# Latent attention on one core: rotated queries first, the query norm's root later, two value blocks to a PSUM bank

## The chip, the core and the metric

The kernel runs on one core of a Trainium2 chip. The metric is the device time of one execution in microseconds. Before the change the median of three runs is 2636.99 us (2633.98 to 2645.04).

## The reference

The program computes two blocks of layers on 512 tokens of width 1024, all in float32. The first is attention beside a state-space layer between two feed-forward layers; the second starts with latent attention (MLA), then layer norms, a convolutional feed-forward layer, a gated linear attention and again the same tail. The change touches the latent attention alone:

```python
def mla_mixer(x, positions, cos, sin, w_in, q_norm, kv_norm, w_uq, w_uk, w_uv, w_o):
    h = x @ w_in
    c_q, c_kv, k_r = jnp.split(h, [MLA_Q_LORA, MLA_Q_LORA + MLA_KV_LORA], axis=-1)
    c_q = rms_norm(c_q, q_norm)
    c_kv = rms_norm(c_kv, kv_norm)
    q = (c_q @ w_uq).reshape(B, S, MLA_HEADS, MLA_NOPE + MLA_ROPE)
    q_nope = q[..., :MLA_NOPE]
    q_rope = apply_rope(q[..., MLA_NOPE:], cos[:, :, None], sin[:, :, None])
    k_rope = apply_rope(k_r, cos, sin)
    k_nope = (c_kv @ w_uk).reshape(B, S, MLA_HEADS, MLA_NOPE)
    v = (c_kv @ w_uv).reshape(B, S, MLA_HEADS, MLA_V)
    scale = (MLA_NOPE + MLA_ROPE) ** -0.5
    ...
    s = (q_nope . k_nope + q_rope . k_rope) * scale, masked, softmax, times v
    ...
    return (o @ w_o).astype(x.dtype)
```

There are 16 heads, with 128 plain and 64 rotated columns in a query and 128 in a value; the query's latent width is 512, that of keys and values 256.

## The kernel before

Every product of float32 matrices is made of three: each operand is split into a high half (a cast by ScalarE to the matmul's format) and a low half (what is left, a subtraction by VectorE), and TensorE adds high x high, high x low and low x high into one PSUM bank (`mm3`, L581 to L583). So a result that is used as an operand again costs a cast on ScalarE and a subtraction on VectorE that both read its bank. Weights come by DMA from SP's queue into `raw`, and are split the same way into `uh` (L554, ScalarE) and `ul` (L569, VectorE), called in the code by `feed_hi` and `feed_lo`, some units ahead of their use.

The code is written out per engine: `latent_pe`, `latent_act` and `latent_dve` each loop over a step i and issue that engine's instructions in the order of the code, with semaphore waits between the engines. An engine never passes an instruction that waits. The steps are a pipeline over the 16 heads: step i has the scores of head i, the transposes of the probabilities of head i-2 and the output of head i-3. Each even step i below 16 starts with the queries and keys of pair p = i/2 of heads.

What TensorE does in an even step from 4 on (one pair, i even):

- `queries_pe`: the plain queries of both heads (`qn` 0 and 1, 12 products each), the rotated queries of both heads in one product (`qr`, 12), the keys of both heads (`kn` 0 and 1, 6 each);
- `latent_output_pe`: the output of head i-3 (`mo`, L2587, 4 products with the weight loads of float32 shown as 8);
- values of pair i/2 - 1, in four blocks of 128 tokens (`lin_tok`, 8 x 3 products of 256 columns), each block in a bank of its own;
- `latent_turn_pe`: ten transposes into three banks (L2559: four, four, two);
- `latent_scores_pe`: the scores of head i, five products for each of four token blocks, in banks 4 to 7.

Everything but the scores rotates through banks 0 to 3 (`bk.limit(4)`, `bk.take`): a group takes the next bank in turn, so it waits until the group four takes before it has been read by the engine that frees it. The readers and what frees a bank: `qn`: cast to `QNH` on ScalarE (L2450), then `QNL` on VectorE (L2474), which frees it. `qr`: four copies of 32 rows on ScalarE (`rope_act`, L2329) which swap the halves, then on VectorE the multiply by the cosine (L2336), which frees it, the multiply by the sine (L2338) and the sum (L2340); the result is cast to `QA` on ScalarE (L2462) and its low half made on VectorE (L2486), and the scores wait for that. `kn`: `KNH` (L2454), then `KNL` (L2479), which frees it. `mo`: `OH` (L2597), then `OL` (L2601), which frees it. Values: the copy to `VT` on ScalarE (L2498). Transposes: copies to `PTm` on VectorE (L2579) and ScalarE (L2577).

ScalarE and VectorE begin the step with the softmax of an earlier head (`latent_softmax_act` L2537; `latent_normalise_dve` L2543 and L2547, `latent_softmax_dve` L2527 and L2530), then the casts of `queries_act`, `OH`, then `queries_turned_act` (`QA`), the weights, `VT`, and `PTm`. In pair 0 the norm of the queries' latent is computed beside the queries: TensorE adds squares between the products (L2361), ScalarE takes the root (`query_norm_act`, L2392) and VectorE the inverse (L2423, L2425), which the softmax multiplies with. After step 10's values half of the output projection is done (`latent_project_pe`), and the other half behind the loop.

Of the kernel before, what the change touches and what calls it, by code (L numbers as in the profile page):

```python
# [22 lines left out]
H2 = [(0, 512)]  # L23
# [245 lines left out]
def program(nc, A, out):  # L269
    with ExitStack() as ctx:  # L270
# [10 lines left out]
        s_mm = tally("s_mm")  # L281

        s_whi, s_hi, s_fn, s_cp = (tally(n) for n in ("s_whi", "s_hi", "s_fn", "s_cp"))

        s_wlo, s_lo, s_par, s_dv = (tally(n) for n in ("s_wlo", "s_lo", "s_par", "s_dv"))
# [33 lines left out]
        bk = Banks(8)  # L319
# [219 lines left out]
        def feed_hi(e, name, ahead=1):  # L539

            u = done["act use"]
            assert units[u].name == name, (units[u].name, name)
            done["act use"] += 1
            ahead_hi(e, ahead)
# [12 lines left out]
        def feed_lo(e, name, ahead=1):  # L557

            u = done["dve use"]
            assert units[u].name == name, (units[u].name, name)  # L560
            done["dve use"] += 1
            ahead_lo(e, ahead)
# [10 lines left out]
        def next_unit(e, name):  # L573
            u = done["pe"]
            assert units[u].name == name, (units[u].name, name)
            done["pe"] += 1
            s_wlo.wait_ge(e, ("unit", u))
            return u

        def mm3(e, o, wh, wl, xh, xl, first, last):  # L580
            e.matmul(o, wh, xh, start=first, stop=False)  # L581
            e.matmul(o, wh, xl, start=False, stop=False)  # L582
            return e.matmul(o, wl, xh, start=False, stop=last)  # L583

        def lin(e, name, X, halves, key, xs=None, cols=None, u=None, frees=True, along=None):

            if u is None:
                u = next_unit(e, name)
            hi, lo, _ = halves_of(u)
            kc = units[u].kc  # L590
            w0, w1 = cols or (0, hi.shape[2])
            xh, xl, tag = X
            for hf, (t0, n) in enumerate(halves):
                b = bk.take(e, key + (hf,))
                for k in range(kc):
                    x = k if xs is None else xs[k]
                    s_lo.wait_ge(e, (tag, x))
                    if along:
                        along()
                    i = mm3(e, psum[0:w1 - w0, b, 0:n], hi[:, k, w0:w1], lo[:, k, w0:w1], xh[:, x, t0:t0 + n],  # L600
                            xl[:, x, t0:t0 + n], k == 0, k == kc - 1)
                ends = [("unit", u)] if frees and hf == len(halves) - 1 else []
                i.then_inc(*s_mm.up(key + (hf,), *ends))
            return u
# [168 lines left out]
        def P(key, n=512, parts=slice(0, 128)):  # L773
            return psum[parts, bk.of[key], 0:n]
# [1539 lines left out]
        def cq_over(e):  # L2314

            s_mm.wait_ge(e, ("cq", 3, 0))
            s_lo.wait_ge(e, ("xq", 3))
            s_fn.wait_ge(e, ("xq", "sq", 3))
# [4 lines left out]
        def rope_act(e, key):  # L2323

            s_mm.wait_ge(e, key)
            if key[0] == "qr" and key[1] > 2:
                s_dv.wait_ge(e, ("rope", "qr", key[1] - 3, 0))
            for k in range(4):
                e.copy(rope_tile(key)[32 * k:32 * k + 32, :], P(key, 512, slice(32 * (k ^ 1), 32 * (k ^ 1) + 32))).then_inc(  # L2329
                    *s_cp.up(("rope",) + key))  # L2330

        def rope_dve(e, key, dst):
            s = rope_tile(key)
            s_cp.wait_ge(e, ("rope",) + key)
            s_par.wait_ge(e, "trig")
            e.tensor_tensor(dst, P(key), COS[:, :], MUL).then_inc(*bk.free(s_dv, key))  # L2336
            s_dv.wait_ge(e, NOW)
            e.tensor_tensor(s, s, SIN[:, :], MUL).then_inc(*s_dv.up())  # L2338
            s_dv.wait_ge(e, NOW)
            e.tensor_tensor(dst, dst, s, ADD).then_inc(*s_dv.up(("rope",) + key))  # L2340
# [49 lines left out]
        def query_norm_act(e):  # L2390
            s_mm.wait_ge(e, "qss")
            e.activation(rq, P("qss", 4), ACT.Sqrt, bias=EPS5, scale=1.0 / 512).then_inc(*bk.free(s_fn, "qss", "qrt"))  # L2392
# [39 lines left out]
                e.tensor_tensor(HV[:, k, :], HV[:, k, :], R0, MUL).then_inc(*s_pool.up(("x0", k)))  # L2432

        def queries_pe(e, p, along=None):
            u = lin(e, "uq", XQ, H2, ("qn", p, 0), cols=(0, 128), frees=False)
            lin(e, "uq", XQ, H2, ("qn", p, 1), cols=(128, 256), u=u, frees=False)
            lin(e, "uq", XQ, H2, ("qr", p), cols=(256, 384), u=u)
            u = lin(e, "uk", XK, H2, ("kn", p, 0), cols=(0, 128), frees=False, along=along)
            lin(e, "uk", XK, H2, ("kn", p, 1), cols=(128, 256), u=u, along=along)

        def queries_act(e, p):
            feed_hi(e, "uq", 2)
            if p:
                s_mm.wait_ge(e, ("ms", 2 * p - 1))
            else:
                cq_over(e)
                s_pool.wait_ge(e, ("x0", 7))
            for hh in range(2):
                s_mm.wait_ge(e, ("qn", p, hh, 0))
                e.copy(QNH[:, hh, :], P(("qn", p, hh, 0))).then_inc(*s_hi.up(("qn", p, hh)))  # L2450
            rope_act(e, ("qr", p, 0))
            for hh in range(2):
                s_mm.wait_ge(e, ("kn", p, hh, 0))
                e.copy(KNH[:, hh, :], P(("kn", p, hh, 0))).then_inc(*s_hi.up(("kn", p, hh)))  # L2454
            if p == 0:
                query_norm_act(e)

        def queries_turned_act(e, p):
            s_dv.wait_ge(e, ("rope", "qr", p, 0))
            for hh in range(2):  # L2460
                rows = slice(64 * hh, 64 * hh + 64)
                e.copy(QA[rows, hh, :], QR[rows, :]).then_inc(*s_hi.up(("qr", p, hh)))  # L2462
            feed_hi(e, "uk", 1 if p == 1 else 2)

        def queries_dve(e, p):
            feed_lo(e, "uq", 2)
            if p:
                s_mm.wait_ge(e, ("ms", 2 * p - 1))
            else:
                cq_over(e)  # L2470
                s_lo.wait_ge(e, "KR")
            for hh in range(2):
                s_hi.wait_ge(e, ("qn", p, hh))
                e.tensor_tensor(QNL[hh][:, :], P(("qn", p, hh, 0)), QNH[:, hh, :].bitcast(F32), SUB).then_inc(  # L2474
                    *bk.free(s_lo, ("qn", p, hh, 0), ("qn", p, hh)))
            rope_dve(e, ("qr", p, 0), QR)
            for hh in range(2):
                s_hi.wait_ge(e, ("kn", p, hh))
                e.tensor_tensor(KNL[:, hh, :], P(("kn", p, hh, 0)), KNH[:, hh, :].bitcast(F32), SUB).then_inc(  # L2479
                    *bk.free(s_lo, ("kn", p, hh, 0), ("kn", p, hh)))  # L2480

        def queries_turned_dve(e, p):
# [4 lines left out]
                    *s_lo.up(("qr", p)))  # L2487
            feed_lo(e, "uk", 1 if p == 1 else 2)

        def latent_values_act(e, p):  # L2490
            feed_hi(e, "uv")
            if p:
                s_mm.wait_ge(e, ("mo", 2 * p - 1))
            else:
                cq_over(e)
            for i in range(4):
                s_mm.wait_ge(e, ("uv", p, i))
                e.copy(VT[:, i, :], P(("uv", p, i), 256)).then_inc(*bk.free(s_cp, ("uv", p, i), ("uv", p)))  # L2498

        def latent_scores_pe(e, h):  # L2500
            p, hh = h // 2, h % 2
# [148 lines left out]
        def latent_pe(e):  # L2650
            latent_first_pe(e)
            bk.limit(4)
            norm = query_norm_pe(e)

            def sums(n):
                for _ in range(n):
                    next(norm, None)

            for i in range(18):
                if i % 2 == 0 and i < 16:  # L2660
                    queries_pe(e, i // 2, None if i else lambda: sums(2))
                if i >= 3:
                    latent_output_pe(e, i - 3)
                if i == 0:
                    lin_tok(e, ("uv",), XK, [0, 128, 256, 384], 256, ("uv", 0), lambda: sums(1))
                if i % 2 == 0 and 4 <= i <= 16:
                    lin_tok(e, ("uv",), XK, [0, 128, 256, 384], 256, ("uv", i // 2 - 1))
                if i == 10:
                    latent_project_pe(e, 0)
                if 2 <= i <= 17:  # L2670
                    latent_turn_pe(e, i - 2)
                if i < 16:
                    latent_scores_pe(e, i)
            bk.limit(8, 4)
            latent_project_pe(e, 1)
            first_layer_pe(e, "h1", "x10", "mo", (OH, OL, "o1"), [("mproj", 1, k) for k in LAST], 0)
# [1051 lines left out]
```

## Time and profile before

| what | value |
|---|---|
| median of three runs | 2636.99 us |
| profiled execution | 2637.52 us |
| its span, first to last instruction | 2635.7 us |
| TensorE (PE) busy | 2573.6 us, 98% |
| its weight loads (PEld) busy | 2214.4 us, 84% |
| VectorE (DVE) busy | 1675.4 us, 64% |
| ScalarE (ACT) busy | 1051.2 us, 40% |
| GpSimd (POOL) busy | 352.6 us, 13% |
| mean DMA rate | 96 GB/s |
| granted TensorE clock, mean | 0.998 of full speed |

The span lies 1.8 us under the profiled execution's own time, and that 0.5 us over the median. The shares are means over stages of very different kinds: the heads' loop of the latent attention takes from about 1226 to 1503 us, with its output projection's first half in it. Within it a busy time of 98% says little: one must look for the idle time just ahead of an instruction, which stands in brackets behind its row together with the work that ended it.

### The profile page before, as it was taken

How to read it: one execution, taken by the hardware profiler on the slowest of the kernel's cores; microseconds unless marked ns; L12 is line 12 of the kernel's file. 1: busy time of each engine (PE TensorE's matmuls, PEld its weight loads, DVE VectorE, ACT ScalarE, POOL GpSimd, SP SyncE). 2: the span in 40 equal slices, each digit the busy share in tenths (PEclk: the TensorE clock that was granted, in tenths of full speed). 3: DMA queues.
4: the chain of work that ended last, by engine and by line, in shares of the span. 5: the costliest groups of instructions: out<-in, count | busy, mean ns of one | idle time of the engine just before them, and what ended most of it. 6: DMA issues, size and time to landing. Idle time of an engine off the chain costs nothing.

```text
span 2635.7 us, 35250 instructions
## 1 busy us (share of the span) xinstructions
PE 2573.6 (98%) x14532; PEld 2214.4 (84%) x14532; DVE 1675.4 (64%) x2597; ACT 1051.2 (40%) x1689; POOL 352.6 (13%) x385
## 2 busy tenths in 40 slices
PE   7999999999999999999999999999999999999999
PEld 7999999976688888887788798888898879888887
DVE  6865864468656534536775777747765477764765
ACT  4222333134434222235562545424454355433435
POOL 1143531220001000011000050000222014000031
PEclk9999999999999999999999999999999999999999
DMA  5243444631133233322121222332332222242322
GB/s 150 89 134 118 135 148 148 218 97 37 48 112 100 80 115 101 92 80 69 44 69 56 69 89 88 96 102 83 109 103 86 75 80 75 78 120 96 92 92 65
DMA packets 297687, 252.91 MB, mean 96 GB/s; under 512 B 20653, under 2 KB 286391, under 8 KB 297527
## 3 DMA queue, kind: packets, MB, share of 16 engines
q1 hardware_dynamic: 286055, 230.76, 27.9%
q0 software_dynamic: 7024, 17.74, 2.3%
q8 instruction: 115, 1.88, 0.3%
q10 hardware_dynamic: 4448, 2.16, 0.3%
q14 instruction: 45, 0.37, 0.0%
HBM read 235.06 MB, written 17.66 MB: 96 GB/s over the span
## 4 chain that ended last, share of the span: by engine, by line
PE 83%; DVE 10%; ACT 4%; issue 2%; POOL 1%; DMA 1%; SPq 0%; ACTq 0%; POOLq 0%; DVEq 0%
PE ps L581 25%; PE ps L582 25%; PE ps L583 25%; DVE ul L569 2%; ACT uh L554 1%; PE ps L2587 1%; PE ps L787 1%; PE ps L2559 1%; PE ps L1660 1%; PE ps L1902 0%; PE ps L2000 0%; DVE rbuf L802 0%; DVE HL L1153 0%; DVE tmp L1142 0%; DVE tmp L2978 0%
## 5 line engine op out<-in xcount | busy, mean ns | idle before, releaser
L569 DVE TENSOR_TENSOR ul<-raw,uh 128x1024 fp32r<-128x1024 f32 (+3 forms) x416 | 513.8, 1258 | 316.2 <-ACT uh L554 315.5
L581 PE MATMUL ps<-OH,uh 128*128 128x512 f32 (+1 forms) x1736 | 645.5, 372 | 4.5 <-DVE ul L569 3.8
L583 PE MATMUL ps<-OH,ul 128*128 128x512 f32 (+1 forms) x1736 | 638.5, 368 | 0.0
L582 PE MATMUL ps<-OL,uh 128*128 128x512 f32 (+1 forms) x1736 | 638.4, 368 | 0.0
L554 ACT CAST uh<-raw 128x1024 fp32r<-128x1024 f32 (+3 forms) x416 | 412.5, 1025 | 157.3 <-PE ps L583 116.9
L581 PEld LDWEIGHTS ps<-OH,uh 128*128 128x128 f32 x1736 | 327.3, 189 | 65.4 <-DVE ul L569 5.6
L582 PEld LDWEIGHTS ps<-OL,uh 128*128 128x128 f32 x1736 | 327.5, 189 | 54.8 <-issue 1.9
L583 PEld LDWEIGHTS ps<-OH,ul 128*128 128x128 f32 x1736 | 327.3, 189 | 54.6
L581 PE MATMUL ps<-HH,uh 128*128 128x512 f32 (+2 forms) x946 | 320.2, 338 | 4.0 <-DVE ul L569 2.9
L582 PE MATMUL ps<-HL,uh 128*128 128x512 f32 (+2 forms) x946 | 318.1, 336 | 0.0
L583 PE MATMUL ps<-HH,ul 128*128 128x512 f32 (+2 forms) x946 | 318.0, 336 | 0.0
L581 PE MATMUL ps<-XH,uh 128*128 128x264 f32 (+1 forms) x992 | 309.5, 312 | 6.2 <-DVE tmp L1146 2.5
L582 PE MATMUL ps<-XL,uh 128*128 128x264 f32 (+1 forms) x992 | 303.5, 306 | 0.0
L583 PE MATMUL ps<-XH,ul 128*128 128x264 f32 (+1 forms) x992 | 303.3, 306 | 0.0
L581 PEld LDWEIGHTS ps<-XH,uh 128*128 128x128 f32 x992 | 186.8, 188 | 25.9 <-issue 14.0
L581 PEld LDWEIGHTS ps<-HH,uh 128*128 128x128 f32 x946 | 178.9, 189 | 24.9 <-DVE ul L569 3.1
L582 PEld LDWEIGHTS ps<-HL,uh 128*128 128x128 f32 x946 | 179.0, 189 | 18.3 <-issue 0.5
L583 PEld LDWEIGHTS ps<-HH,ul 128*128 128x128 f32 x946 | 179.0, 189 | 18.2
L583 PEld LDWEIGHTS ps<-XH,ul 128*128 128x128 f32 x992 | 187.0, 189 | 8.4
L582 PEld LDWEIGHTS ps<-XL,uh 128*128 128x128 f32 x992 | 187.0, 189 | 7.1
L818 POOL TENSOR_TENSOR acc<-acc,tmp 128x512 f32<-128x512 f32 (+2 forms) x56 | 69.4, 1239 | 668.3 <-ACT tmp L808 664.0
L2752 POOL TENSOR_TENSOR acc<-H 128x512 f32<-128x512 f32 x4 | 8.6, 2147 | 939.3 <-DVE H L2991 621.2
(471 smaller groups left out, 3725.7 us busy)
## 6 DMA issues: line engine op xcount, KB each, us to landing
raw<-in_ffn_w SPq DMA_DIRECT2D x40, 1024.0 KB, 5.1
raw<-in_ffn_w_up SPq DMA_DIRECT2D x40, 1024.0 KB, 5.0
raw<-in_ffn_w SPq DMA_DIRECT2D x32, 704.0 KB, 4.3
raw<-in_ffn_w_down SPq DMA_DIRECT2D x32, 704.0 KB, 4.4
raw<-in_w_in SPq DMA_DIRECT2D x16, 1024.0 KB, 5.6
raw<-in_gla_w_in SPq DMA_DIRECT2D x12, 1024.0 KB, 5.0
raw<-in_mla_w_o SPq DMA_DIRECT2D x8, 1024.0 KB, 4.7
raw<-in_ple_w_gate SPq DMA_DIRECT2D x8, 1024.0 KB, 4.8
```

What stands on the lines that cost most here:

```text
L554: e.copy(h, src).then_inc(*s_whi.up((u, j)))
L569: e.tensor_tensor(l, src, h.bitcast(F32), SUB).then_inc(*s_wlo.up(("unit", u)))
L581: e.matmul(o, wh, xh, start=first, stop=False)
L582: e.matmul(o, wh, xl, start=False, stop=False)
L583: return e.matmul(o, wl, xh, start=False, stop=last)
L787: i = e.matmul(psum[:, b, 0:n], ones[:, :], tile[:, t0:t0 + n], start=j == 0, stop=j == len(parts) - 1)
L818: e.tensor_tensor(a, a, tmps[k - 1][:, t0:t0 + n], ADD).then_inc(*s_pool.up(*((tag, "acc", k, hf) for hf in hfs)))
L1660: t = e.matmul(psum[:, b, 66 * g:66 * g + 66], w[:, 128 * g:128 * g + 128], UB[q][:, e0 + g, :], start=True, stop=True)
L2559: t = e.transpose(psum[:, b, o:o + 128], SS[h % 2][:, SO[n] + 128 * k:SO[n] + 128 * k + 128], ident[:, :])
L2587: t = e.matmul(psum[:, b, 128 * k:512], VT[:, k, 128 * (h % 2):128 * (h % 2) + 128], PTm[:, PO[k]:PO[k] + 512 - 128 * k], start=k == 0, st ...
L2752: e.tensor_tensor(a, HV[:, 0, :], HV[:, 1, :], ADD).then_inc(*s_pool.up((xt, "two")))
```

## The change

Three edits, all in the loop over pairs of heads. First, `qr` is made ahead of `qn` 0 and 1 on TensorE, and read ahead of them on ScalarE and VectorE (`rope_act` and `rope_dve` stand first). Second, the root of the query norm moves on ScalarE from behind pair 0's key casts to behind its `QA` casts. Third, two blocks of values share a bank (`latent_values_pe`): the unit, the products and their sizes stay, but only two banks are taken and `VT` is filled by two copies of 512 columns in place of four of 256.

```diff
         def queries_pe(e, p, along=None):
-            u = lin(e, "uq", XQ, H2, ("qn", p, 0), cols=(0, 128), frees=False)
-            lin(e, "uq", XQ, H2, ("qn", p, 1), cols=(128, 256), u=u, frees=False)
-            lin(e, "uq", XQ, H2, ("qr", p), cols=(256, 384), u=u)
+            u = lin(e, "uq", XQ, H2, ("qr", p), cols=(256, 384), frees=False)
+            lin(e, "uq", XQ, H2, ("qn", p, 0), cols=(0, 128), u=u, frees=False)
+            lin(e, "uq", XQ, H2, ("qn", p, 1), cols=(128, 256), u=u)
...
         def queries_act(e, p):
             feed_hi(e, "uq", 2)
+            if p == 0:
+                cq_over(e)
+                s_pool.wait_ge(e, ("x0", 7))
+            rope_act(e, ("qr", p, 0))
             if p:
                 s_mm.wait_ge(e, ("ms", 2 * p - 1))
-            else:
-                cq_over(e)
-                s_pool.wait_ge(e, ("x0", 7))
             for hh in range(2):
                 s_mm.wait_ge(e, ("qn", p, hh, 0))
                 e.copy(QNH[:, hh, :], P(("qn", p, hh, 0))).then_inc(*s_hi.up(("qn", p, hh)))
-            rope_act(e, ("qr", p, 0))
...
-            if p == 0:
-                query_norm_act(e)

         def queries_turned_act(e, p):
...
+            if p == 0:
+                query_norm_act(e)
             feed_hi(e, "uk", 1 if p == 1 else 2)

         def queries_dve(e, p):
             feed_lo(e, "uq", 2)
+            if p == 0:
+                cq_over(e)
+                s_lo.wait_ge(e, "KR")
+            rope_dve(e, ("qr", p, 0), QR)
             if p:
                 s_mm.wait_ge(e, ("ms", 2 * p - 1))
-            else:
-                cq_over(e)
-                s_lo.wait_ge(e, "KR")
             for hh in range(2):
                 s_hi.wait_ge(e, ("qn", p, hh))
...
-            rope_dve(e, ("qr", p, 0), QR)
...
+        def latent_values_pe(e, p, along=None):
+            u = next_unit(e, "uv")
+            hi, lo, _ = halves_of(u)
+            xh, xl, tag = XK
+            for j in range(2):
+                b = bk.take(e, ("uv", p, j))
+                for a in range(2):
+                    t0 = 256 * j + 128 * a
+                    for k in range(2):
+                        s_lo.wait_ge(e, (tag, k))
+                        if along:
+                            along()
+                        t = mm3(e, psum[:, b, 256 * a:256 * a + 256], xh[:, k, t0:t0 + 128], xl[:, k, t0:t0 + 128],
+                                hi[:, k, 0:256], lo[:, k, 0:256], k == 0, k == 1)
+                t.then_inc(*s_mm.up(("uv", p, j), *([("unit", u)] if j else [])))
...
-            for i in range(4):
-                s_mm.wait_ge(e, ("uv", p, i))
-                e.copy(VT[:, i, :], P(("uv", p, i), 256)).then_inc(*bk.free(s_cp, ("uv", p, i), ("uv", p)))
+            for j in range(2):
+                s_mm.wait_ge(e, ("uv", p, j))
+                e.copy(VT[:, 2 * j:2 * j + 2, :].rearrange("p a n -> p (a n)"), P(("uv", p, j))).then_inc(
+                    *bk.free(s_cp, ("uv", p, j), ("uv", p)))
```

How the order of instructions changes, at three places. Line numbers behind the new function are 17 higher in the changed kernel.

ScalarE, pair 0, from the weight casts to the copies of the values (`misc` is the norm's column, `tmp` the rotation's tile):

```order
 L554 CAST uh<-raw_53 128x512
-L2450 CAST QNH<-ps 128x512 x2
 L2329 COPY tmp_65<-ps 32x512 x4
+L2451 CAST QNH<-ps 128x512 x2
 L2454 CAST KNH<-ps 128x512 x2
+L2460 CAST QA<-tmp_61 64x512 x2
 L2392 ACTIVATE misc<-ps,misc 128x4
-L2462 CAST QA<-tmp_61 64x512 x2
 L554 CAST uh<-raw_54 128x4x256
 L554 CAST uh<-raw_54 128x4x128
-L2498 COPY VT<-ps 128x256 x4
```

The rotated copies move ahead of the query casts, and the root behind the casts of QA.

VectorE, pair 0 (every pair has the same move; `tmp_61` is the rotated query):

```order
 L569 TENSOR_TENSOR ul<-raw_53,uh 128x512
-L2474 TENSOR_TENSOR QNL_163<-ps,QNH 128x512
-L2474 TENSOR_TENSOR QNL_164<-ps,QNH 128x512
 L2336 TENSOR_TENSOR tmp_61<-ps,COS 128x512
 L2338 TENSOR_TENSOR tmp_65<-tmp_65,SIN 128x512
 L2340 TENSOR_TENSOR tmp_61<-tmp_61,tmp_65 128x512
+L2475 TENSOR_TENSOR QNL_163<-ps,QNH 128x512
+L2475 TENSOR_TENSOR QNL_164<-ps,QNH 128x512
 L2479 TENSOR_TENSOR KNL<-ps,KNH 128x512 x2
```

The two low halves of the plain queries now stand behind the three operations of the rotation.

TensorE, pair 2 (step 4) of the changed kernel, from the last key product to the transposes, with the semaphores that a row waits for (`s_dv`: VectorE's results that no product takes as a low half, `s_lo`: its low halves, `s_cp`: ScalarE's copies):

```order
L581 MATMUL ps<-CKH,uh 128x512 [waits s_dv]
...
L2604 MATMUL ps<-PTm,VT 128x512 [waits s_lo]
...
L581 MATMUL ps<-uh,CKH 128x256 [waits s_lo,s_wlo]
...
L2576 MATMUL ps<-ident,SS_166 128x128 [waits s_lo]
L2576 MATMUL ps<-ident,SS_166 128x128 x3
L2576 MATMUL ps<-ident,SS_166 128x128 [waits s_lo]
L2576 MATMUL ps<-ident,SS_166 128x128 x3
L2576 MATMUL ps<-ident,SS_166 128x128 [waits s_cp]
```

Before, the first of these rows waited for `s_lo` and all three groups of transposes for `s_cp`. Now the last key product takes the bank of `qr`, freed by the cosine multiply; the output takes the bank of `qn` 0, freed by its low half; the first two groups of transposes take those of `kn` 1 and `mo`, and the third that of the first two value blocks, freed by their copy.

## Rows read from the trace of the kernel before

**Rows 1.** The page's part 4: the chain that ended last, share of the span by engine.
```profile
PE 83%; DVE 10%; ACT 4%; issue 2%; POOL 1%; DMA 1%; SPq 0%; ACTq 0%; POOLq 0%; DVEq 0%
```

**Rows 2.** Stages: stretch, length, busy us (x instructions) by engine, clock, DMA.
```profile
core 0: us, PE busy (x) PEld busy (x) DVE busy (x) ACT busy (x) POOL busy (x), PEclk, DMA share, GB/s
1240.00:1500.00 260.00, 247.18 (x1317) 208.17 (x1317) 186.48 (x363) 135.60 (x316) 0.00 (x0) 0.99 0.17 57
```

**Rows 3.** Waits of TensorE, 1190 to 1560 us: total us, times, longest.
```profile
PE ps L581 <- DVE QA L2486: 3.4, 2, 1.8
PE ps L2559 <- ACT VT L2498: 3.3, 4, 0.8
```

**Rows 4.** Timelines of pair 0: start, length, instruction, idle before; then its clock.
```profile
1229.71 0.59 ACT L2450 CAST QNH<-ps 128x512 fp32r<-128x512 f32 x1
...
1243.86 0.26 ACT L2392 ACTIVATE misc<-ps,misc 128x4 f32<-128x4 f32 x1 [3.58 <-PE ps L2361]
1244.02 1.24 ACT L2462 CAST QA<-tmp 64x512 fp32r<-64x512 f32 x2
...
1246.11 0.38 PE L581 MATMUL ps<-KNH,QNH 128*128 128x256 f32 x1 [1.84 <-DVE QA L2486]
...
1246.00:1248.00 2.00, 1.89 (x14) 1.89 (x15) 1.70 (x3) 1.98 (x7) 0.00 (x0) 1.00 0.03 8
```

**Rows 5.** Timelines of pair 1.
```profile
1261.62 1.06 ACT L2450 CAST QNH<-ps 128x512 fp32r<-128x512 f32 x2
...
1263.71 0.50 PE L581 MATMUL ps<-CKH,uh 128*128 128x512 f32 x1 [0.86 <-DVE QNL L2474]
...
1268.49 1.40 DVE L2486 TENSOR_TENSOR QA<-tmp,QA 64x512 fp32r<-64x512 f32 x2
```

**Rows 6.** Timelines of pair 2, and the same stop one pair on.
```profile
1286.34 1.06 ACT L2450 CAST QNH<-ps 128x512 fp32r<-128x512 f32 x2
1288.12 2.38 ACT L2329 COPY tmp<-ps 32x512 f32<-32x512 f32 x4 [0.72 <-PE ps L583]
...
1292.99 0.59 ACT L2597 CAST OH<-ps 128x512 fp32r<-128x512 f32 x1 [1.39 <-PE ps L2587]
...
1296.24 1.18 ACT L2498 COPY VT<-ps 128x256 f32<-128x256 f32 x4
...
1290.53 0.69 DVE L2336 TENSOR_TENSOR tmp<-ps,COS 128x512 f32<-128x512 f32 x1 [2.09 <-ACT tmp L2329]
...
1292.60 1.28 DVE L2479 TENSOR_TENSOR KNL<-ps,KNH 128x512 fp32r<-128x512 f32 x2
1293.79 0.68 DVE L2601 TENSOR_TENSOR OL<-ps,OH 128x512 fp32r<-128x512 f32 x1
...
1300.01 0.34 DVE L2527 SCALAR_TENSOR_TENSOR SS<-ps,misc,MK 128x128 f32<-128x128 f32 x1
...
1289.28 0.39 PE L581 MATMUL ps<-CKH,uh 128*128 128x512 f32 x1
...
1290.64 2.32 PE L2587 MATMUL ps<-PTm,VT 128*128 128x512 f32 x8
...
1296.65 1.31 PE L2559 MATMUL ps<-ident,SS 128*128 128x128 f32 x10 [0.83 <-ACT VT L2498]
...
1324.40 1.31 PE L2559 MATMUL ps<-ident,SS 128*128 128x128 f32 x10 [0.82 <-ACT VT L2498]
```

**Rows 7.** Timelines of steps 16 and 17, and the clock between.
```profile
1496.21 0.39 PE L581 MATMUL ps<-uh,CKH 128*128 128x256 f32 x1 [2.27 <-DVE OL L2601]
...
1497.03 2.29 PE L2559 MATMUL ps<-ident,SS 128*128 128x128 f32 x10
1499.12 3.00 PE L2587 MATMUL ps<-PTm,VT 128*128 128x512 f32 x8
1501.96 1.26 PE L2559 MATMUL ps<-ident,SS 128*128 128x128 f32 x10
...
1496.41 1.22 DVE L569 TENSOR_TENSOR ul<-raw,uh 128x1024 fp32r<-128x1024 f32 x1 [0.26 <-ACT uh L554]
...
1498.00:1499.00 1.00, 1.00 (x7) 0.96 (x6) 0.69 (x1) 0.06 (x1) 0.00 (x0) 0.50 0.00 0
```

More of the change, by code:

```diff
@@ L2664, in latent_pe @@
                 if i == 0:
-                    lin_tok(e, ("uv",), XK, [0, 128, 256, 384], 256, ("uv", 0), lambda: sums(1))
+                    latent_values_pe(e, 0, lambda: sums(1))
                 if i % 2 == 0 and 4 <= i <= 16:
-                    lin_tok(e, ("uv",), XK, [0, 128, 256, 384], 256, ("uv", i // 2 - 1))
+                    latent_values_pe(e, i // 2 - 1)
                 if i == 10:
```

## The prediction

> **What bounds the kernel now.** I read the chain of waits first: TensorE is 83% of it, VectorE 10% [rows 1]. Then the stretch that the change touches, 1240 to 1500 us, in the table of stages: TensorE is busy 247.18 of 260 us [rows 2], so all its idle time there is 12.8 us, 0.49% of the 2637 us. Nothing that only removes waits of TensorE in this stretch can give more. Then who makes TensorE wait: first of all the low half of the rotated query (QA, 3.4 us) and the copies of the values (VT, 3.3 us) [rows 3]. About 0.5% is also what a measurement of this kernel can tell from no change. Last I read the timelines of three places: pair 0, pair 1, one steady pair (pair 2 stands for 3, 4 and 6, whose stop is the same 0.82 or 0.83 us), and the end of the loop.
>
> What decides is not in one row: the rotating four banks. A product may start only when the group four takes back has been read. Before, the group of the output (mo) took the bank of the second query head, read by L2474 ahead of the rotation. Now it takes the bank of the first head, read on VectorE behind all three operations of the rotation. The last key product (kn1) takes the bank of the rotated queries.
>
> **The change part by part.** TensorE's instructions are the same, in another order, so they cost nothing by themselves. Four copies of 256 columns (1.18 us for four [rows 6]) become two of 512 (two such casts take 1.06 us [rows 6]); 0.1 us of ScalarE, hidden. No DMA is added, and nothing on SP or GpSimd moves. The sum:
>
> Pair 0. The root waited for its sum until 1243.86, with the QA casts behind it (1.24 us), and TensorE stood 1.84 us for the low half of QA until 1246.11 [rows 4]. Now the rotated copies start where QNH did, at 1229.71; with 2.38 us for them and 2.07 for VectorE's three steps (both from rows 6) the rotation is done by about 1234.3, and the QA casts run as soon as the key casts are through, ahead of the root's sum. The root is behind them and still starts at 1243.86. TensorE's stop goes, but what VectorE and ScalarE do next (weight halves, softmax) follows the root, and moves up only by the 1.24 us of the casts. The second head's scores wait for softmax to free their banks, so TensorE keeps **1.24 us** and no more.
>
> Pair 1. ScalarE reaches the pair late, so the rotated copies (2.38 us) start at 1261.62 less 1.24, that is 1260.4. The multiply is done at 1263.5, and kn1 starts at about 1263.6 where it was 1263.71 [rows 5]: a stop of 2.0 us in place of 0.86 (TensorE gets there 1.24 earlier, and leaves 0.11 earlier). The copies end at 1262.8; VectorE's three steps take 2.07, its four low halves 2.4 to 2.5 (0.6 each, two in a row 1.28 [rows 6]), so QA starts at 1267.4 where it was 1268.49. Of the 1.24 us, **-1.1** is left.
>
> Steady pair (times of pair 2). ScalarE is free at 1286.34. Before, it cast both query heads and then waited 0.72 us for the rotated product; the output began at 1290.64 with no stop, and only the transposes stood 0.83 us for VT [rows 6]. Now: rotated copies 1286.34 to 1288.72; multiply done at 1288.75 + 0.69 = 1289.44, kn1 wanted at 1289.28, a stop of 0.2. VectorE's three rotation steps take 2.07 us (1290.53 to 1292.60), so QNL of head 0 starts at 1290.82, is done at 1291.50, and the output starts at 1291.55: **0.9 us late**. OH follows the output's start by 2.35 us (1292.99 less 1290.64), so 1294.0 with 0.1 for a pipeline that restarts; OL follows the end of OH, 1294.0 + 0.59 + 0.03 = 1294.62 instead of 1293.79, that is +0.83. VT follows OH by 3.25 us: 1297.25, and its first copy ends at 1297.83. The first eight transposes no longer wait for VT, the last two do: they end at about 1298.1, where all ten ended at 1297.7. So TensorE loses 0.4 in the first such pair. VectorE has 6.2 us of unbroken work from OL to the next softmax (1300.01 less 1293.79), then softmax, exponentials and casts hand on to the next rotation without TensorE. So +0.83 per pair becomes the loop's own delay, and TensorE follows it: the period goes from 27.75 us (1296.65 to 1324.40) to 28.6.
>
> Pairs 2 to 5: 4 x 0.83 = **+3.3** (pair 5 hands it to the projection's first weight half, which is also behind QA on VectorE). In the projection VectorE catches up, so pair 6 starts clean: **+0.7**. Pair 7: **+0.83**.
>
> The end. TensorE stopped 2.27 us for OL before the last value product, and then its clock was at 0.50, so that output 14 took 3.00 us [rows 7] and not 2.32 [rows 6]. Now both banks of values are free, and eight products and four transposes run before OL is needed. Output 14 then waits for VectorE: its weight half (1496.41, 1.22 us) and the first of two copies of transposes (0.6 us) end at 1498.2, so it starts there (before 1499.12), is passed at 1500.3 at full clock, and the transposes behind it stand there instead of at 1501.96: **-1.5**.
>
> Sum: -1.1 + 3.3 + 0.7 + 0.83 - 1.5 = **+2.2 us**. On the profiled execution's 2637.52 this is 2639.7; the median of the runs is 0.53 lower, so 2639.2.
>
> The cost that no row shows is the clock after the new, more frequent stops. One stop of 1.84 us was followed by 1.00 of the clock, one of 2.27 by 0.50 [rows 4, 7]. So a new stop of 2.0 us (pair 1) lies between the two ends: nothing, or about 1.7 us (the excess of output 14, 3.00 less 2.32, and of the ten transposes ahead of it, 2.29 less 1.31 [rows 6, 7]). I take nothing, since it is nearest to 1.84 and VectorE sets the pace there.
>
> The Trainium skill, "TensorE: Matmul & The Clock Gate", section "A second HAM failure mode: psum-queue depth-cycling", speaks against such a change: cycling through PSUM banks lets TensorE idle briefly between groups often enough that its clock swings between its two levels. The trace so far does not bear it out for stops of 0.8 to 1.8 us.
>
> **The rivals.** (a) The bank waits are hidden after all (a copy sooner, or the loop has slack I don't see). Then pairs 2, 3, 4 and 6 lose their 0.82 and the end its 1.5, on top of 1.1: 1.1 + 3.3 + 1.5 = 5.9 us faster, 2631. For it: VectorE stands 2.09 us before the rotation, which was the longest idle of its pair [rows 6]. Against: that idle only moves to before OL. (b) Slower by more than can be hidden: the clock falls to half in the new stops of each pair. It decides when the stops at kn1 and at the output, close together, act as the 2.27 us one did. Eight pairs at 1.7 us are 13.6, with 2.2 of the sum 15.8: 2652.8. Against it: the largest new stop outside pair 1 is about 1 us, and 1.84 us did nothing. This is what that rule of the Trainium skill would come to here. (c) The order changes nothing that the loop notices: the loop is as long as before, only pair 0 and the end count, 1.1 + 1.5 = 2.6 us faster, 2634.4. That TensorE's pace would be unaffected needs the output's bank read no later than now, and the order of instructions says otherwise.
>
> **How the numbers follow.** My forecast 0.62, (a) 0.2, (b) 0.05, (c) 0.13. The forecast's own range is 2636 to 2643 (0.4 to 1.2 us per pair for the loop's delay). To hold 8 in 10 the range takes in (c) and most of (a), and leaves (b) out: 2631 to 2644. More than 0.5% faster, below 2623.8, would need all idle time of the stretch gone and the slow clock too: 0.02. Slower than 2650.2 is (b): 0.05. Within: 0.93.
>
> **What would show it.** In the changed profile: no stop before pair 0's scores; the rotated copies directly behind the weight casts; in pairs 2, 3 and 4 a stop before kn1 (rotation's multiply) and one of about 0.6 to 0.9 us before the output, ended by QNL (L2475); the stop before the transposes moved to the last two; a period of 28.6 us; the clock at 1.00 at the end of the loop. A period of 26.9 to 27.8 us would prove the forecast wrong and (a) or (c) right; a granted clock under 0.95 over 1240 to 1500 would speak for (b).

## The result and the profile after

The changed kernel takes 2641.99 us (median of 20 executions, 2639.52 to 2646.91) where the kernel before took 2635.53 us (20 executions, 2633.57 to 2645.04): a ratio of 1.0019, 95% interval 1.0013 to 1.0025, so 3.4 to 6.6 us slower; the two medians by themselves differ by 6.46 us. That is less than the 0.5% bound of the prediction: no change that matters, but one of known sign. The forecast was 2639.2 us, +2.2.

| | before | after |
|---|---|---|
| profiled execution's span | 2635.7 us | 2643.4 us |
| TensorE busy | 2573.6 us | 2582.6 us |
| VectorE busy | 1675.4 us | 1675.7 us |
| ScalarE busy | 1051.2 us | 1050.8 us |

The work is the same, so the place has to be found. The stretch that the change touches can be cut out of both traces exactly: it begins with the first query product and ends at the same 0.70 us stop in the second half of the projection. The two kernels' rows (timelines of TensorE, before and then after):

```profile
1226.42 0.50 PE L581 MATMUL ps<-CQH,uh 128*128 128x512 f32 x1 [0.34 <-DVE ul L569]
...
1514.98 0.50 PE L581 MATMUL ps<-OH,uh 128*128 128x512 f32 x1 [0.70 <-DVE OL L2601]
```

```profile
1228.24 0.50 PE L581 MATMUL ps<-CQH,uh 128*128 128x512 f32 x1 [0.33 <-DVE ul L569]
...
1522.08 0.50 PE L581 MATMUL ps<-OH,uh 128*128 128x512 f32 x1 [0.70 <-DVE OL L2618]
```

Before it is 288.56 us long and after 293.84: **+5.28 us**, as much as the ratio says (0.19% of 2636 is 5.0). The remaining 2.4 us by which the spans differ lie in code that is the same in both, 1.8 of them ahead of the stretch. From here on each kernel's stretch is compared with the 288.56 us, since that is free of such differences. It is still one traced execution of each kernel, and the executions of one kernel scatter by more than that (the 20 of the kernel before by 11 us), so the runs' ratios are given beside it.

The chain of waits and the stages, in answer to [rows 1] and [rows 2]:

```profile
PE 80%; DVE 12%; ACT 5%; issue 2%; POOL 1%; DMA 1%; SPq 0%; ACTq 0%; POOLq 0%; DVEq 0%
```

```profile
1240.00:1500.00 260.00, 249.07 (x1306) 206.06 (x1305) 183.12 (x356) 131.01 (x291) 0.00 (x0) 0.99 0.17 57
```

TensorE's share of the chain falls from 83 to 80%, and VectorE's and ScalarE's rise: more of the loop is now paced by them. "Busy" misleads here. TensorE is busier in the 260 us than before (249.07 against 247.18) with fewer instructions (1306 against 1317), and over the two stretches its idle time is nearly the same, 13.5 us before and 13.7 after. Matmuls at half clock count as busy, but they are not the main part: a steady pair at full clock has 27.51 us of busy time in its 28.80 us, where it had 26.92 in 27.75 for the same 149 products (table of stages, from the stop before the transposes of pair 2 to that of pair 3). Part of what a stop costs is shown as busy. In pair 3 the product behind the stop before kn1 starts 1.13 us after the one ahead of it (1319.20 less 1318.07), where 0.23 us is usual; that is 0.90 us late for a bracket of 0.74, and its own row is 0.50 us long instead of 0.39. So the places below are compared by the distance from start to start, not by idle time.

The waits of TensorE (total us, times, longest), for [rows 3]:

```profile
PE ps L581 <- DVE tmp L2336: 5.2, 6, 2.0
...
PE ps L2604 <- DVE QNL L2475: 2.4, 6, 0.4
PE ps L2576 <- DVE OL L2618: 1.0, 1, 1.0
PE ps L2604 <- DVE PTm L2596: 1.0, 1, 1.0
PE ps L581 <- DVE QA L2486: 0.9, 1, 0.9
...
PE ps L2576 <- ACT VT L2514: 0.7, 4, 0.2
```

The wait for VT fell from 3.3 to 0.7 us and the one for QA from 3.4 to 0.9, as meant. Two took their place that the kernel before did not have in this form: for the cosine multiply L2336 (the bank that kn1 takes) and for QNL (the bank that the output takes), 7.6 us together, of which 2.0 are the one stop of pair 1.

Pairs 0 and 1 (timelines of ScalarE and TensorE, then the clock of one stage), for [rows 4, 5]:

```profile
1241.99 1.26 ACT L2460 CAST QA<-tmp 64x512 fp32r<-64x512 f32 x2
...
1245.67 0.26 ACT L2392 ACTIVATE misc<-ps,misc 128x4 f32<-128x4 f32 x1 [2.42 <-PE ps L2361]
...
1249.52 0.39 PE L581 MATMUL ps<-KNH,QNH 128*128 128x256 f32 x1 [0.19 <-DVE SS L2544]
...
1265.43 0.50 PE L581 MATMUL ps<-CKH,uh 128*128 128x512 f32 x1 [2.02 <-DVE tmp L2336]
1265.77 0.40 PE L582 MATMUL ps<-CKL,uh 128*128 128x512 f32 x1
...
1270.71 0.39 PE L581 MATMUL ps<-KNH,QNH 128*128 128x256 f32 x1 [0.91 <-DVE QA L2486]
...
1265.00:1268.00 3.00, 2.57 (x8) 1.90 (x9) 2.93 (x6) 1.37 (x4) 0.00 (x0) 0.69 0.73 258
```

QA is cast ahead of the root, and the 1.84 us stop is gone. Pair 1 has the forecast stop of 2.0 us before kn1, and its scores begin 42.47 us into the stretch (1270.71 less 1228.24) where they began at 43.52: -1.05 us. Behind that stop the clock fell (0.69 in the mean from 1265 to 1268 us).

A steady pair (pair 3; ScalarE, VectorE, TensorE), for [rows 6], with the same stop one pair sooner as the last row:

```profile
1316.03 2.39 ACT L2329 COPY tmp<-ps 32x512 f32<-32x512 f32 x4
1318.45 1.07 ACT L2451 CAST QNH<-ps 128x512 fp32r<-128x512 f32 x2
...
1323.71 0.59 ACT L2614 CAST OH<-ps 128x512 fp32r<-128x512 f32 x1 [2.22 <-PE ps L2604]
...
1326.95 1.06 ACT L2514 COPY VT<-ps 128x512 f32<-128x512 f32 x2
...
1318.45 0.69 DVE L2336 TENSOR_TENSOR tmp<-ps,COS 128x512 f32<-128x512 f32 x1 [1.64 <-ACT tmp L2329]
...
1320.52 1.28 DVE L2475 TENSOR_TENSOR QNL<-ps,QNH 128x512 fp32r<-128x512 f32 x2
...
1324.33 0.69 DVE L2618 TENSOR_TENSOR OL<-ps,OH 128x512 fp32r<-128x512 f32 x1 [1.34 <-ACT OH L2614]
...
1330.64 0.34 DVE L2544 SCALAR_TENSOR_TENSOR SS<-ps,misc,MK 128x128 f32<-128x128 f32 x1
...
1319.20 0.50 PE L581 MATMUL ps<-CKH,uh 128*128 128x512 f32 x1 [0.74 <-DVE tmp L2336]
...
1321.25 2.42 PE L2604 MATMUL ps<-PTm,VT 128*128 128x512 f32 x8 [0.38 <-DVE QNL L2475]
...
1327.59 0.44 PE L2576 MATMUL ps<-ident,SS 128*128 128x128 f32 x2 [0.17 <-ACT VT L2514]
...
1298.79 0.44 PE L2576 MATMUL ps<-ident,SS 128*128 128x128 f32 x2 [0.17 <-ACT VT L2514]
```

This is the ring of waits step by step. The rotated copies start at once; the output starts 5.22 us behind them, when QNL of head 0 (1320.52 + 0.68) has freed its bank; OH follows 2.46 us later, OL 0.62, the next softmax 6.31, and 14.19 us after that the next pair's rotated copies (1344.83). The sum is 28.80 us, and so is the distance of the two stops before the last transposes (1327.59 less 1298.79). Before it was 27.75. In pair 2, the first of its kind, the stop before kn1 is 0.20 us; from pair 3 on it is about 0.74, and in pair 6, behind the projection, there is none.

The end of the loop, for [rows 7]:

```profile
1503.07 1.15 PE L2576 MATMUL ps<-ident,SS 128*128 128x128 f32 x6 [1.03 <-DVE OL L2618]
1505.24 3.99 PE L2604 MATMUL ps<-PTm,VT 128*128 128x512 f32 x8 [1.03 <-DVE PTm L2596]
...
1506.00:1507.00 1.00, 1.00 (x2) 0.34 (x1) 0.82 (x3) 0.00 (x0) 0.00 (x0) 0.50 0.07 16
```

The stages from pair 2 to step 16 of the same kernel, for comparison:

```profile
1272.00:1500.00 228.00, 220.42 (x1151) 181.86 (x1150) 159.71 (x312) 111.85 (x251) 0.00 (x0) 1.00 0.18 59
```

There the clock is whole. At the end one stop of 2.27 us became two of 1.03, and the clock was halved all the same: the output took 3.99 us.

### The profile page after: what moved, and what is told of

Read it like the earlier page. It is cut to its first block, busy times and chain, and to the rows that moved or that the text cites. A ratio compares the mean times of both kernels' runs of the same rounds, so it can differ in the third digit from the quotient of the medians.

```text
span 2643.4 us, 35223 instructions
## 1 busy us (share of the span) xinstructions
PE 2582.6 (98%) x14532; PEld 2218.0 (84%) x14532; DVE 1675.7 (63%) x2597; ACT 1050.8 (40%) x1673; POOL 353.0 (13%) x385
## 4 chain that ended last, share of the span: by engine, by line
PE 80%; DVE 12%; ACT 5%; issue 2%; POOL 1%; DMA 1%; SPq 0%; ACTq 0%; POOLq 0%; DVEq 0%
PE ps L581 25%; PE ps L583 24%; PE ps L582 24%; DVE ul L569 2%; ACT uh L554 2%; PE ps L2604 1%; DVE zst L2547 1%; DVE SS L2544 1%; PE ps L787 1%; PE ps L1660 1%; ACT tmp L2329 1%; DVE SS L2564 1%; PE ps L1902 0%; PE ps L2000 0%; DVE PTm L2596 0%
```

## The experiments

My theory: three things add up. The root's move frees pair 0 of its stop; the value banks shorten each steady pair; the order of the queries makes the output wait for a bank behind the rotation, and this costs more than both give. The clock of TensorE takes or returns a microsecond or two on top. The main rival: the value banks are the loss. All eight kernels were timed against the kernel before in five rounds. e1 to e4 ran on one chip and e5 to e9 on another, each beside the kernel before on the same chip.

| kernel | ratio to before, 95% interval | stretch by the trace | against before | up to the output of step 16 | from there to the end |
|---|---|---|---|---|---|
| before | | 288.56 us | | 263.06 us | 25.50 us |
| the change | 1.0019 (1.0013 to 1.0025) | 293.84 us | +5.28 | 268.17 | 25.67 |
| e1, values only | 0.9986 (0.9978 to 0.9995) | 284.58 us | -3.98 | 260.34 | 24.24 |
| e2, order and root | 1.0015 (1.0006 to 1.0023) | 292.72 us | +4.16 | 268.48 | 24.24 |
| e3, root only | 1.0001 (0.9992 to 1.0010) | 288.63 us | +0.07 | 264.29 | 24.34 |
| e4, root and values | 0.9992 (0.9983 to 1.0001) | 285.73 us | -2.83 | 261.50 | 24.23 |
| e5, QNL inside the rotation | 1.0002 (0.9994 to 1.0011) | 289.76 us | +1.20 | 264.02 | 25.74 |
| e6, the change, end filled | 1.0012 (1.0003 to 1.0021) | 292.58 us | +4.02 | 268.50 | 24.08 |
| e8, e4 with stops filled | 0.9977 (0.9966 to 0.9988) | 283.27 us | -5.29 | 259.04 | 24.23 |
| e9, e3 with pair 1 filled | 0.9985 (0.9977 to 0.9994) | 286.10 us | -2.46 | 261.75 | 24.35 |

The last two columns split the stretch at the start of step 16's output. Behind that point the traces fall into two groups: 24.1 to 24.4 us where TensorE's clock stayed at full speed, and 25.5 to 25.7 where it was halved for a while (the kernel before, the change, e5). So the kernel before has 1.2 us of slow clock of its own there, and whoever compares whole stretches with it counts that as a gain of the edit. What an edit does to the loop is read from the column before it.

### e1: only the value banks

The kernel before, with `latent_values_pe` and the two copies of the third edit.

```diff
-            for i in range(4):
-                s_mm.wait_ge(e, ("uv", p, i))
-                e.copy(VT[:, i, :], P(("uv", p, i), 256)).then_inc(*bk.free(s_cp, ("uv", p, i), ("uv", p)))
+            for j in range(2):
+                s_mm.wait_ge(e, ("uv", p, j))
+                e.copy(VT[:, 2 * j:2 * j + 2, :].rearrange("p a n -> p (a n)"), P(("uv", p, j))).then_inc(
+                    *bk.free(s_cp, ("uv", p, j), ("uv", p)))
```

> The kernel before with only the third edit, two value blocks to a bank. My theory (the loss comes from the order of the queries, the value banks only help): the query banks are read as before, so there is no stop before the output; only the last two transposes of a steady pair wait for the first value copy, and the stop before them falls from 0.83 us to some 0.3, the period from 27.75 us to about 27.2. Four such pairs and the end give -2 to -3.5 us in all (-0.1%). The rival (the value banks are the loss, since a bank with two blocks is read later): a period over 27.75 us and a time of +3 us or more.

The stops before the last transposes of two pairs, and the end of the loop (TensorE's timeline of e1):

```profile
1293.04 0.44 PE L2576 MATMUL ps<-ident,SS 128*128 128x128 f32 x2 [0.17 <-ACT VT L2514]
...
1320.12 0.44 PE L2576 MATMUL ps<-ident,SS 128*128 128x128 f32 x2 [0.16 <-ACT VT L2514]
...
1489.77 1.14 PE L2576 MATMUL ps<-ident,SS 128*128 128x128 f32 x6 [1.20 <-DVE OL L2618]
1491.94 2.39 PE L2604 MATMUL ps<-PTm,VT 128*128 128x512 f32 x8 [1.03 <-DVE PTm L2596]
```

The period is 27.08 us, 0.67 less than before, and no pair stops before the output. Up to step 16's output the edit gains 2.72 us, four pairs at 0.67. The other 1.26 of the 3.98 us come at the end, and nearly all of that is the clock, which stays at full speed here (an output of 2.39 us): with four value banks and the full clock (e3, e9) the end takes 24.34 us, with two banks 24.24. So the edit itself is worth 2.8 us, inside the range expected. The rival falls.

### e2: order and root, values in four banks

The changed kernel with the third edit taken back.

> The changed kernel with the values back in four banks: rotated queries first and the root late remain. My theory: the output still takes the bank of query head 0, so the period is 28.8 us as with the whole change, and the time +5 to +6.5 us (+0.2%) over before. The rival (the value banks are the loss): the period is 27.75 us or less, and the time within 1 us of before.

Two steady pairs (TensorE's timeline of e2):

```profile
1321.22 2.42 PE L2587 MATMUL ps<-PTm,VT 128*128 128x512 f32 x8 [0.40 <-DVE QNL L2475]
...
1327.34 1.31 PE L2559 MATMUL ps<-ident,SS 128*128 128x128 f32 x10 [0.82 <-ACT VT L2498]
...
1350.02 2.42 PE L2587 MATMUL ps<-PTm,VT 128*128 128x512 f32 x8 [0.40 <-DVE QNL L2475]
```

The period is 28.80 us (1350.02 less 1321.22), with the value banks and without them. So once the order is changed the value banks give next to nothing (268.17 us up to step 16's output against 268.48 without them): TensorE's old wait for VT, 0.82 us, is still there and harmless, since the ring that sets the pace does not run through it. The +4.16 us are a little under what I gave; its end came out at full clock (an output of 2.39 us), unlike the change's.

### e3: the root alone

```diff
@@ queries_act
-            if p == 0:
-                query_norm_act(e)
@@ queries_turned_act
+            if p == 0:
+                query_norm_act(e)
             feed_hi(e, "uk", 1 if p == 1 else 2)
```

> The kernel before with the root of the query norm moved behind pair 0's QA casts, and nothing else. My theory: in the old order the rotation is also done by 1239.7, so the root alone removes the 1.84 us stop of pair 0, and -1.1 to -1.3 us stay; the periods stay 27.75 us. The rival (pair 0's gain comes from the rotation being early): the stop stays above 1.5 us, and the time is unchanged.

The stop went, yet the time stayed. The timeline of TensorE in pair 1, the clock of one stage and the end of the loop of e3; then pair 1 and the same stage of before:

```profile
1269.31 0.58 PE L581 MATMUL ps<-KNH,QNH 128*128 128x256 f32 x1 [1.59 <-DVE QA L2486]
...
1275.16 1.02 PE L2587 MATMUL ps<-PTm,VT 128*128 128x512 f32 x2
...
1268.00:1271.00 3.00, 1.69 (x8) 1.69 (x9) 2.90 (x8) 0.58 (x2) 0.00 (x0) 0.52 0.00 0
...
1498.08 0.39 PE L581 MATMUL ps<-uh,CKH 128*128 128x256 f32 x1 [2.26 <-DVE OL L2601]
...
1500.44 2.40 PE L2587 MATMUL ps<-PTm,VT 128*128 128x512 f32 x8 [0.29 <-ACT PTm L2577]
```

```profile
1269.94 0.39 PE L581 MATMUL ps<-KNH,QNH 128*128 128x256 f32 x1 [1.59 <-DVE QA L2486]
...
1273.27 2.32 PE L2587 MATMUL ps<-PTm,VT 128*128 128x512 f32 x8
...
1268.00:1271.00 3.00, 1.41 (x10) 1.17 (x11) 2.91 (x6) 1.19 (x3) 0.00 (x0) 1.00 0.00 0
```

Into the stretch, e3's scores of pair 1 begin at 42.25 us (1269.31 less 1227.06), 1.27 earlier than before: the root alone has all of pair 0's gain, and the order has no part in it. But they take 5.85 us to the output instead of 3.33, at half the clock: 2.5 us lost. Both kernels had the same three stops in pair 1 (0.87, 1.40 and 1.59 us here; 0.86, 1.40 and 1.59 before). The rest came back at the end, where e3's output took 2.40 us and before's 3.00, after a stop of the same length (2.26 and 2.27 us). My sum was right for the place and wrong for the whole, and only e9 could say whether the clock was the reason.

### e4: root and values, the old order

> The kernel before with the second and third edit, without the first: old order of queries. My theory: the gains of both add, -3 to -5 us (about -0.15%), with no stop before kn1 or before the output in pairs 2 to 7 and a period of about 27.2 us: a version that beats both kernels. The rival (the order is needed for them): no better than before.

-2.83 us by the stretch, -0.08% by the runs with an interval that just reaches no change. Better than the changed kernel, but by the stretch worse than e1 alone and just short of the 3 to 5 us expected: the scores of pair 1 begin at 1265.32 and their output at 1271.10, 5.78 us, the same loss to the clock as in e3. The period is 27.1 us, and there is no stop before kn1 or the output from pair 2 on.

### e5: QNL made inside the rotation

The changed kernel; on VectorE both QNL stand between the cosine and the sine multiply. TensorE and ScalarE keep the changed order.

```diff
         def rope_dve(e, key, dst, between=lambda: None):
             ...
             e.tensor_tensor(dst, P(key), COS[:, :], MUL).then_inc(*bk.free(s_dv, key))
+            between()
             s_dv.wait_ge(e, NOW)
             e.tensor_tensor(s, s, SIN[:, :], MUL).then_inc(*s_dv.up())
```

> The changed kernel, with VectorE making both QNL between the cosine multiply and the sine multiply of the rotation instead of behind the sum. Nothing else differs. My theory (the output waits for the bank of query head 0): QNL of head 0 is done some 1.3 us sooner, the 0.4 us stop before the output goes, the stop before kn1 (0.75 us) stays, and the period falls from 28.80 us to 28.1 to 28.3: 3 to 4 us faster than the changed kernel, so +1 to +2 us over before. The rival (the loop's delay is in the rotated copies standing first on ScalarE, not in the bank): a period of 28.7 us or more and +5 us.

A steady pair (TensorE's timeline of e5):

```profile
1318.24 0.50 PE L581 MATMUL ps<-CKH,uh 128*128 128x512 f32 x1 [0.73 <-DVE tmp L2336]
1319.75 2.32 PE L2608 MATMUL ps<-PTm,VT 128*128 128x512 f32 x8
...
1325.97 0.44 PE L2580 MATMUL ps<-ident,SS 128*128 128x128 f32 x2 [0.16 <-ACT VT L2518]
```

The stop before the output is gone, the one before kn1 is as it was, and the period is 28.13 us (1325.97 less 1297.84), 0.67 less than the change's. By the runs the kernel is back at before's time (1.0002), by the stretch it is 4.08 us shorter than the change. The gain lies in the loop (264.02 against 268.17 us up to step 16's output), and the clock has no part in it: both kernels' ends are slow (25.74 and 25.67). So **the bank behind the rotation costs 4.1 us**; it is shown and not only argued. That is not most of what the order costs. The two other edits without the order, with the clock kept up in pair 1, come to step 16's output at 259.04 us (e8, below) and the change at 268.17, so the order costs 9.1 us, of which the gains of the root and the value banks hide 4.0. The 5.0 us that e5 still lacks are one microsecond per pair over e1's 27.08 us, and the only new stop left in its pairs is the one before kn1 (0.72 to 0.75 us, as the trace counts it), the other bank that the order moved. No run took that stop away, so this half is argued from the trace.

### e6: the change, with the stops at the end filled

```diff
+        def filler(e, n):
+            s_dv.wait_ge(e, ("bank", ("ms", 15, 0)))
+            for _ in range(n):
+                e.matmul(psum[:, 4, 0:512], QNH[:, 0, 0:128], QNH[:, 0, :], start=True, stop=True)
```

> The changed kernel, with ten products into a bank that nobody reads added in the two stops at the end of the loop (five before the second group of transposes of step 16, five before the output of step 17); they add work whose result is not used. My theory (the end's gain was eaten by the half clock): the clock stays at 1.00, the output of step 17 takes 2.3 to 2.4 us instead of 3.99, and the kernel is 1.5 to 1.9 us faster than the changed one, +3.5 us over before. The rival (the end is held by VectorE, the clock costs nothing): the time is that of the changed kernel or worse, +5.3 us.

The output in step 17 and the clock behind it (e6):

```profile
1505.30 2.39 PE L2611 MATMUL ps<-PTm,VT 128*128 128x512 f32 x8
...
1506.00:1507.00 1.00, 1.00 (x4) 0.50 (x3) 0.88 (x3) 0.00 (x0) 0.00 (x0) 1.00 0.00 0
```

The clock stayed, the output took 2.39 us and the end fell from 25.67 to 24.08 us, as expected. The stretch fell by only 1.26 us, since in this run every step from pair 1 on came 0.3 to 0.4 us later. The ratio went from 1.0019 to 1.0012; the intervals overlap, so by the runs alone not even the direction is certain.

The later steps teach something too. Up to the end of the loop e6 issues the instructions of the changed kernel, and kn1 of pair 1 starts at the same 37.19 us into the stretch, after the same stop of 2.02 us. But the clock fell sooner: the second product of kn1 took 0.63 us where it took 0.40 in the changed kernel (e6):

```profile
1265.66 0.63 PE L582 MATMUL ps<-CKL,uh 128*128 128x512 f32 x1
```

The keys came later by this, VectorE waited 0.29 us for KNH, and the scores began at 42.86 us instead of 42.47.

### e9 and e8: the stops of pair 1 filled

Both add 14 products of `CQH` with itself into bank 4, whose scores have been read: three before kn1, five before the third group of transposes and six before the scores of pair 1; e8 has nine more at the end. Their results are not used.

> The root alone (the kernel of e3) with the same 14 unused products in pair 1. My theory (the root's 1.2 us was gained and lost again to the clock in pair 1): the scores of pair 1 take 3.3 us and not 5.85, and the time is 1 to 2.5 us below before. The rival (the root gains nothing): within 0.3 us of before.

e9 is e3 with them. Into the stretch, its scores of pair 1 begin at 42.26 us (1265.80 less 1223.54), as in e3, and now at full clock:

```profile
1266.00:1269.00 3.00, 3.00 (x20) 2.83 (x20) 2.90 (x10) 0.18 (x1) 0.00 (x0) 1.00 0.02 5
```

The stretch falls by 2.53 us against e3, to -2.46, and the runs say -0.15%. So the half clock was what had hidden the root's gain. Of the -2.46, 1.31 are there at step 16's output; the rest is the end, which e9 passes at full clock without any fill, as e3 did, and the kernel before at half.

> Root and values (the kernel of e4) with 14 such unused products in the three stops of pair 1 and 9 in the two at the end. My theory: e4 lost 2.5 us to a half clock in pair 1, so here the scores of pair 1 take 3.3 us and not 5.8, and the time is 2.3 to 2.8 us below e4's, about -5 us (-0.2%) against before. The rival (the slow scores of pair 1 in e4 have another cause, or the fill gets in the way): no faster than e4, or the pairs' starts come later by the length of the fill.

e8 is e4 with them (TensorE's timeline of e8 in pair 1; the scores take 3.31 us where e4's took 5.78):

```profile
1266.42 0.39 PE L581 MATMUL ps<-KNH,QNH 128*128 128x256 f32 x1 [0.20 <-DVE QA L2488]
...
1269.73 2.32 PE L2615 MATMUL ps<-PTm,VT 128*128 128x512 f32 x8
```

The stretch is 2.46 us shorter than e4's. The median of its executions is 2630.28 us against 2635.95 for the kernel before on the same chip: 0.23% faster, interval 0.12 to 0.34%. 4.0 of the 5.29 us are gained up to step 16's output, the rest at the end. It beats both kernels, with two of the three edits and 23 products that compute nothing.

## Why the prediction was right

The range held, the sign of the forecast was the measured one, and in the loop the mechanism was the one foretold: the output waits for the bank read behind the rotation, and the delay repeats with every pair. The size was not: forecast +2.2 us, +5.28 in the stretch. That 2641.99 us still lies inside 2636 to 2643 owes something to the width of that range, which allowed 0.4 to 1.2 us per pair (measured 1.05), and something to luck: the kernel before came out 1.5 us lower in twenty executions than in the three that I had added to. Of the missing 3.1 us the ring makes 1.3 and the end 1.7. Term by term, as times into the stretch:

- **Pairs 0 and 1**, -1.1: the trace shows -1.05. The stop before kn1 was forecast at 2.0 us and is 2.02. The clock did fall there, for which I had taken nothing, and in this execution it cost nothing, because VectorE works without a break from 1264.69 us to the low half of QA, as argued. It was close: in e6, where the clock fell sooner at the same place, it cost 0.39 us. I had credited the order of the queries with part of pair 0's gain; e3 shows that the root's move has it all.
- **Pairs 2 to 5**, 4 x 0.83 = +3.3: the projection's first half starts at 157.19 us (1385.43 less 1228.24) against 154.04, so with the -1.05 these pairs cost 4.2. This term was sized too small. I took the shift of OL in one pair and let it repeat; the ring's true length is 28.80 us, not 28.6. The difference lies in links that I had taken from the kernel before: 6.31 us for 6.22 between OL and the softmax, and 14.19 for 14.09 between the softmax and the rotated copies. The second is all between ScalarE's weight casts and what follows them (1.14 us to the first rotated copy, before 1.04 to the first QNH cast). Why either is longer is not shown. The stop before the output is 0.38 to 0.40 us and not the 0.6 to 0.9 that I had named as a sign; the stop before kn1, forecast at 0.2 and 0.20 in pair 2, grew to 0.74 instead.
- **Pairs 6 and 7**, +0.7 and +0.83: together 1.96. The output of step 16 starts at 268.17 us (1496.41 less 1228.24) against 263.06, +5.11.
- **The end**, -1.5 (my own times, 1500.3 for 1501.96, give 1.7): the trace shows +0.17. This is where the prediction failed. The banks did free TensorE as foretold, and output 14 starts 0.81 us nearer (+4.30 there). But I had counted this output at full clock and so booked the slow clock's cost as regained. The clock was halved again, for longer (an output of 3.99 us, before 3.00), and that took 0.98 us back. Of the forecast 1.5 us the banks alone are worth 0.1 (24.24 against 24.34 us, e1 and e3 at full clock); the rest was the clock. e6 shows that it keeps its speed when the stops are filled.

My guess at the clock, a stop of 1.84 us leaves it alone and one of 2.27 halves it, also fell: e3 and e9 have a stop of 2.26 us at the same place and stay at full speed.

The rival (a), hidden bank waits, is refuted by e2 and e5: the stops before the output are there, and taking them away gives 4.1 us. (b), a clock fallen in every pair, did not come: from pair 2 on the new stops of 0.74 and 0.38 us left the granted clock at 1.00 (the stage from 1272 to 1500 us of the changed kernel). The rule of the Trainium skill that I had put beside it ("TensorE: Matmul & The Clock Gate", "A second HAM failure mode: psum-queue depth-cycling") thus does not describe the steady pairs here; for pair 1 and the end, where stops of 0.9 to 2.0 us stand within a few microseconds of each other, it has a point: e3, e4 and the change lost 1 to 2.5 us each to a halved clock. (c), no effect on the loop, is refuted by the period.

## What to carry to other kernels

Where products rotate through a few PSUM banks, the order in which they are made decides who waits for whose reader: before moving one, write down for each product the group four takes back and what stands ahead of its reader on its engine. When the old wait is removed, look for the next ring: with the order changed, the value banks' gain of 2.7 us in the loop shrank to 0.3, because the ring no longer ran through them. Test the edits of a change one by one; this one held a gain of 2.7 us and one of 1.3, and a loss of 9.1 (268.17 against e8's 259.04 us up to step 16's output). And before a gain is booked to an edit, look whether the clock was the same in both traces: here that alone made 1.2 us at the end of the loop.

## What the runs showed of the hardware

The granted clock does not follow from the length of the stops alone. With the same three stops in pair 1 (0.86 or 0.87, 1.39 or 1.40 and 1.59 or 1.60 us) it stayed at 1.00 in the kernel before and in e1, and fell to half in e3 (0.52 from 1268 to 1271 us) and e4, whose stops come 1.3 us nearer to the start of the stretch. At the end, one stop of 2.27 us halved it in the kernel before, and one of 2.26 in e3 and e9 did not; two stops (1.20 or 1.03, then 1.03 us) left it at full speed in e1 and e4 (an output of 2.39 us) and halved it in the changed kernel and e5 (3.99).

That kernels with the same stops at the same times agree, and that the runs follow the traces (e3 1.0001, e9 0.9985, with intervals that just touch), speaks against an accident of one execution. But each kernel was traced only once, and the moment does vary: the changed kernel and e6, with the same instructions and times up to there, lost the clock about half a microsecond apart in pair 1. What decides is open; it was not tried to move the same stops in time by a known amount, nor to trace one kernel many times. What helped in both places was to leave TensorE no long stop, even with products that nobody reads.

A stop also costs TensorE more than its idle time in the profile. In a steady pair at full clock the three stops of the changed kernel show 0.74, 0.38 and 0.17 us, 0.47 more than the one of 0.82 before, and the pair is 1.05 us longer.
